# The residual kept by tokens in a two-block transformer kernel on one NeuronCore

## The reference

```
x = x + scale * gate * rmsnorm(sublayer(rmsnorm(x, g_in) [* (1+sc) + sh]), g_out)
rmsnorm(x, g) = x / sqrt(mean(x*x over the 1024 features) + eps) * g
order: FFN, attention+SSD, FFN | FFN, RWKV-7 time mix, FFN | gated conv, MoE, delta net, MoE
```

## Time and profile before

| | |
|---|---|
| three executions | 3096.75 us median, 3092.67 to 3099.21 |
| the profiled execution | 3096.22 us, its span 3094.4 us |
| busy in the span | PE 92%, PEld 73%, DVE 42%, ACT 36%, POOL 7% |
| mean granted TensorE clock | 0.955 |
| DMA | 695.31 MB, mean 225 GB/s |

### The profile page before, as it was taken

One profiled execution on the slowest core, in us unless ns is written; L12 is line 12 of the kernel. 1 busy time (PEld: TensorE's weight loads), 2 busy tenths in 40 slices (PEclk: granted clock), 3 DMA queues, 4 the chain that ended last, 5 costly groups with the idle time before them and its releaser, 6 DMA issues.

```text
span 3094.4 us, 44358 instructions
## 1 busy us (share of the span) xinstructions
PE 2850.0 (92%) x18548; PEld 2243.9 (73%) x18548; DVE 1293.7 (42%) x2083; ACT 1121.7 (36%) x1980; POOL 205.5 (7%) x174
## 2 busy tenths in 40 slices
PE   8999878998999998789998999999896979999998
PEld 6879656887878888578797666666695856666665
DVE  5556266546447544455464121212384442212212
ACT  5444245435447222254443122222454242222222
POOL 1000001001000212110010000000102400000000
PEclk9999898999999999899998999999897989999999
DMA  8424655535525111054243799999550035999996
GB/s 339 180 96 164 260 232 226 193 137 190 191 83 204 56 55 55 28 202 179 109 164 150 310 417 418 415 416 414 225 186 14 1 122 227 415 415 417 414 416 252
DMA packets 95540, 695.31 MB, mean 225 GB/s; under 512 B 10592, under 2 KB 10720, under 8 KB 11232
## 3 DMA queue, kind: packets, MB, share of 16 engines
q1 hardware_dynamic: 95328, 692.33, 56.4%
HBM read 691.23 MB, written 1.05 MB: 224 GB/s over the span
## 4 chain that ended last, share of the span: by engine, by line
PE 86%; DVE 5%; ACT 4%; issue 2%; DMA 1%; POOL 0%; SPq 0%; DVEq 0%; ACTq 0%
PE bank L1486 14%; PE bank L741 12%; PE bank L743 12%; PE bank L742 12%; PE bank L1546 7%; PE bank L1464 4%; PE bank L1573 4%; PE bank L1826 2%; PE bank L1834 2%; PE bank L1838 2%; DMA weight_ring<-weight_slots 1%; PE bank L1370 1%; PE bank L1936 1%; PE bank L575 1%; PE bank L2342 1%
## 5 line engine op out<-in xcount | busy, mean ns | idle before, releaser
L1486 PE MATMUL bank<-weight_ring,packed_h 128*64 128x256 f32 x2176 | 285.4, 379 | 0.0
L741 PE MATMUL bank<-source_hi_lo,weight_hi_lo 128*128 128x256 f32 x864 | 253.8, 294 | 11.9 <-DVE source_hi_lo L731 4.9
L1486 PE MATMUL bank<-more_slots,packed_h 128*64 128x256 f32 x1920 | 257.0, 379 | 1.5 <-ACT packed_h L1473 1.5
L741 PE MATMUL bank<-gate_up_hi_lo,x_hi_lo 128*128 128x512 f32 x640 | 254.0, 397 | 0.0
L1486 PEld LDWEIGHTS bank<-weight_ring,packed_h 128*64 128x64 f32 x2176 | 196.5, 137 | 74.0 <-issue 18.1
L743 PE MATMUL bank<-gate_up_hi_lo,x_hi_lo 128*128 128x512 f32 x640 | 249.7, 390 | 0.0
L742 PE MATMUL bank<-gate_up_hi_lo,x_hi_lo 128*128 128x512 f32 x640 | 249.2, 389 | 0.0
L742 PE MATMUL bank<-source_hi_lo,weight_hi_lo 128*128 128x256 f32 x864 | 248.0, 287 | 0.0
L743 PE MATMUL bank<-source_hi_lo,weight_hi_lo 128*128 128x256 f32 x864 | 247.8, 287 | 0.0
L1486 PEld LDWEIGHTS bank<-more_slots,packed_h 128*64 128x64 f32 x1920 | 174.1, 137 | 69.6 <-issue 15.4
L700 DVE TENSOR_TENSOR weight_hi_lo<-weight_ring,weight_hi_lo 128x1024 fp32r<-128x1024 f32 x138 | 168.1, 1222 | 103.9 <-ACT weight_hi_lo L694 103.9
(11 more groups left out here) (546 smaller groups left out, 5548.4 us busy)
## 6 DMA issues: line engine op xcount, KB each, us to landing
weight_ring<-weight_slots SPq DMA_DIRECT2D x437, 1024.0 KB, 7.5
more_slots<-weight_slots SPq DMA_DIRECT2D x212, 1024.0 KB, 9.3
params_sb<-small_params SPq DMA_DIRECT2D x1, 3216.5 KB, 17.8
h_sb<-weight_slots SPq DMA_DIRECT2D x3, 1024.0 KB, 4.9
y_sb<-weight_slots SPq DMA_DIRECT2D x3, 1024.0 KB, 8.3
x_sb<-x_T SPq DMA_DIRECT2D x1, 1024.0 KB, 4.8
out_T<-x_sb SPq DMA_DIRECT2D x4, 256.0 KB, 2.1
params_sb<-small_params SPq DMA_DIRECT2D x1, 73.5 KB, 4.6
```

The costliest lines, as they stand in the source:

```text
L741: e.matmul(out, w[0], x[0], start=start, stop=False, skip_group_check=shared)
L1486: mm = e.matmul(ps[x * CAP:(x + 1) * CAP, m * FB:(m + 1) * FB], self.hc[:, c, (2 * (p % 2) + x) * CAP:(2 * (p % 2) + x + 1) * CAP], wt[:, ...
```

## The change

x lies by tokens (128 x 2 x 1024). y times its inverse times the norm's weights, which now are a row spread over all partitions, is one DVE instruction for each bank, and a second adds it to x. The squares of x are summed along the free axis by ACT in one instruction for each 128 tokens. At the head of each stage PE turns x (FFN) or x times its inverse (others), and ACT (chunks 0 to 3) and DVE (chunks 4 to 7) read the turned x from banks 6, 7, 0 and 1, in pieces of 128x128, with gain and shift applied there.

The rows of weights come as six more slots of 1 MB (`plan_gain`) in the first six stages; in the last four PE spreads them and ACT writes them (`spread_pe`, `spread_act`), before `out_rows_pe` in conv and delta, and before the first gather in MoE. The place of a gain slot is free for the next load when the stage's x is whole (`x_new` of q = 1, f = 1). `out_rows_pe` makes its last two chunks first for banks 0 and 1, then for 2 and 3. The FFN head splits both halves of its first weights on ACT between the pieces of x, and all low parts on DVE. POOL's work at the FFN heads and in delta's (L3567) is gone, and so are `back_pe`, `early_act`, `chunk_act` and the norm's products on PE. The diff, cut to its new lines (the old ones stand above):

```diff
+def gain_slot(g):
+    row = np.zeros((P, SLOT), np.float32)
+    row[:, 0:D] = g
+    return row
...
+        slots.append(gain_slot(a["norm_gains"][layer, 1]))
...
+        self.x, self.h, self.y = sb("x_sb", [P, TT, D]), sb("h_sb", [P, C, T]), sb("y_sb", [P, C, T])
+        by_tokens = lambda m: m[:, :, :].rearrange("p c t -> p (c t)").rearrange("p (q d) -> p q d", q=TT)
+        self.y_tok, self.h_tok = by_tokens(self.h), by_tokens(self.y)
...
+    def x_T(self, q, c):
+        return self.k.bank[(6, 7, 0, 1)[2 * q + c // 4]][:, c % 4 * P:c % 4 * P + P]
+    def turn_in_pe(self, e, src, came, read):
+        k, n = self.k, self.n
+        for q in range(TT):
+            for c in range(C):
+                if c % 4 == 0:
+                    if q == 0:
+                        k.banks.take(e, (n, "turned", c // 4), *read(c + 3), of=(6 + c // 4,))
+                    for signal in came(q, c // 4):
+                        e.wait_ge(*k.ge(*signal))
+                mm = e.transpose(self.x_T(q, c), src[:, q, c * P:(c + 1) * P], k.par("ident"))
+                if c % 4 == 3:
+                    mm.then_inc(*k.up("in_turned", n, q, c // 4))
+    def squares_act(self, e, q):
+        k, n = self.k, self.n
+        if n:
+            e.wait_ge(*k.ge(*self.x_key(q, 1)))
+        e.activation(k.y_tok[:, q, :], k.x[:, q, :], ACT.Square, accum_out=k.x_sums[:, q:q + 1]).then_inc(*k.up("x_squared", n, q))
+        e.wait_ge(*k.ge("x_squared", n, q))
+        e.activation(k.x_dev[:, q:q + 1], k.x_sums[:, q:q + 1], ACT.Sqrt, scale=1.0 / D, bias=k.par("eps", 0, 1)).then_inc(*k.up("x_deviation", n, q))
+    def inverse_of_x_dve(self, e, q):
+        k, n = self.k, self.n
+        e.wait_ge(*k.ge("x_deviation", n, q))
+        e.reciprocal(k.x_inv[:, q:q + 1], k.x_dev[:, q:q + 1]).then_inc(*k.up("x_inverse", n, q))
+    def head_act(self, e):
+        k, n = self.k, self.n
+        for q in range(TT):
+            self.squares_act(e, q)
+            e.wait_ge(*k.ge("x_inverse", n, q))
+            e.activation(k.h_tok[:, q, 0:512], k.x[:, q, 0:512], ACT.Copy, scale=k.x_inv[:, q:q + 1]).then_inc(*k.up("scaled_first", n, q))
+            if q == 0:
+                self.begin(e)
+                self.first_split_act(e)
+    def first_split_act(self, e):
+        self.split_act(e, 0)
+    def first_half_dve(self, e):
+        self.scaled_dve_half(e, 0)
+    def head_dve(self, e):
+        self.scaled_dve_half(e, 1)
+        self.begin(e)
+    def scaled_dve_half(self, e, q):
+        k, n = self.k, self.n
+        self.inverse_of_x_dve(e, q)
+        e.wait_ge(*k.ge("x_inverse", n, q))
+        e.tensor_scalar(k.h_tok[:, q, 512:1024], k.x[:, q, 512:1024], k.x_inv[:, q:q + 1], None, ALU.mult).then_inc(*k.up("scaled_second", n, q))
...
+    def h_key(self, c, q=1):
+        return "h_second" if c // 4 else "h_first", self.n, q, c
     def norm_pe(self, e):
+        n = self.n
+        self.turn_in_pe(e, self.k.h_tok, lambda q, f: (("scaled_second" if f else "scaled_first", n, q),), lambda c: (self.h_key(c, 0),))
...
+    def norm_act(self, e, gain, shift=None, behind=None, between=None):
+        k, n = self.k, self.n
+        for q in range(TT):
+            if q == 0:
+                e.wait_ge(*k.ge("x_squared", n, 1))
+            e.wait_ge(*k.ge("in_turned", n, q, 0))
+            for c in range(4):
+                if shift is None:
+                    e.activation(k.h[:, c, q * P:(q + 1) * P], self.x_T(q, c), ACT.Copy, scale=gain[:, c:c + 1]).then_inc(*k.up(*self.h_key(c, q)))
+                else:
+                    e.activation(k.h[:, c, q * P:(q + 1) * P], self.x_T(q, c), ACT.Identity, scale=gain[:, c:c + 1], bias=shift[:, c:c + 1]).then_inc(*k.up(*self.h_key(c, q)))
+                if q and behind and c:
+                    behind(c - 1)
+            if q == 0 and between:
+                between()
         if behind:
+            for c in range(3, C):
+                behind(c)
+    def norm_dve(self, e, gain, shift=None, behind=None):
+        k, n = self.k, self.n
+        for q in range(TT):
+            e.wait_ge(*k.ge("in_turned", n, q, 1))
+            for c in range(4, C):
+                if shift is None:
+                    e.tensor_scalar(k.h[:, c, q * P:(q + 1) * P], self.x_T(q, c), gain[:, c:c + 1], None, ALU.mult).then_inc(*k.up(*self.h_key(c, q)))
+                else:
+                    e.tensor_scalar(k.h[:, c, q * P:(q + 1) * P], self.x_T(q, c), gain[:, c:c + 1], shift[:, c:c + 1], ALU.mult, ALU.add).then_inc(*k.up(*self.h_key(c, q)))
+        if behind:
             for c in range(C):
+                behind(c)
+    def plan_gain(self):
+        w = self.k.weights
+        self.gain_at = w.take()
+        self.gain_row = w.mem(self.gain_at)[:, 0:D]
+        w.done(self.gain_at, ("x_new", self.n, 1, 1))
+    def gain_in(self):
+        return self.k.weights.landed(self.gain_at)
...
+    def spread_pe(self, e, gain):
+        k, n = self.k, self.n
+        for f in range(2):
+            ps = k.banks.take(e, (n, "gain", f), ("gain_row", n, f))
+            for c in range(4 * f, 4 * f + 4):
+                mm = e.matmul(ps[:, c % 4 * P:c % 4 * P + P], gain[:, c:c + 1].to_broadcast([P, P]), k.par("ident"), start=True, stop=True)
+            mm.then_inc(*k.up("gain_spread", n, f))
+    def spread_act(self, e):
+        k, n = self.k, self.n
+        for f in range(2):
+            e.wait_ge(*k.ge("gain_spread", n, f))
+            e.activation(self.gain_row[:, f * 512:f * 512 + 512], k.banks.at(n, "gain", f)[:, :], ACT.Copy).then_inc(*k.up("gain_row", n, f))
     def back_act(self, e, scale=1.0):
         k, n = self.k, self.n
...
         for q in range(TT):
             for b in (2 * q, 2 * q + 1):
                 e.wait_ge(*k.ge(*self.y_key(b)))
+                e.activation(k.y_tok[:, q, b % 2 * 512:b % 2 * 512 + 512], k.bank[b][:, :], ACT.Square, accum_out=k.y_sums[:, b:b + 1]).then_inc(*k.up("out_squared", n, b))
             e.wait_ge(*k.ge("out_squared", n, 2 * q + 1))
             e.wait_ge(*k.ge("out_part", n, q))
             e.activation(k.y_dev[:, q:q + 1], k.y_sums[:, 2 * q + 1:2 * q + 2], ACT.Sqrt, scale=s2, bias=k.y_part[:, q:q + 1]).then_inc(*k.up("out_deviation", n, q))
         nxt = self.following()
         if nxt:
+            nxt.head_act(e)
+    def back_dve(self, e, gain_in, scale=1.0):
         k, n = self.k, self.n
         s2 = 1.0 / (scale * scale)
         nxt = self.following()
...
             e.wait_ge(*k.ge("out_deviation", n, q))
             e.reciprocal(k.y_inv[:, q:q + 1], k.y_dev[:, q:q + 1]).then_inc(*k.up("out_inverse", n, q))
             e.wait_ge(*k.ge("out_inverse", n, q))
+            for f in range(2):
+                cut = slice(f * 512, f * 512 + 512)
+                if q == 0:
+                    e.wait_ge(*gain_in(f))
+                e.scalar_tensor_tensor(out=k.y_tok[:, q, cut], in0=k.bank[2 * q + f][:, :], scalar=k.y_inv[:, q:q + 1], in1=self.gain_row[:, cut],
+                                       op0=ALU.mult, op1=ALU.mult).then_inc(*k.up("out_scaled", n, q, f))
+            if nxt and q:
+                nxt.first_half_dve(e)
+            for f in range(2):
+                cut = slice(f * 512, f * 512 + 512)
+                e.wait_ge(*k.ge("out_scaled", n, q, f))
+                e.tensor_tensor(k.x[:, q, cut], k.x[:, q, cut], k.y_tok[:, q, cut], ALU.add).then_inc(*k.up("x_new", n, q, f))
         if nxt:
+            nxt.head_dve(e)
...
     def out_rows_pe(self, e, first, tag, chunks=C):
         k, n = self.k, self.n
+        def part(kc, b, end):
+            w = self.units[first + kc][2]
+            tq, cut = slice(b // 2 * P, b // 2 * P + P), slice(b % 2 * 512, b % 2 * 512 + 512)
+            x = self.x_r[:, :, kc, tq]
+            return self.mm3(e, k.bank[b][:, :], (x[:, 0, :], x[:, 1, :]), (w[:, 0, cut], w[:, 1, cut]), kc == 0, end)
+        for kc in range(chunks - 2):
+            e.wait_ge(*k.ge(*self.lo_key(first + kc)))
             e.wait_ge(*k.ge("source_lo", n, tag, kc))
             for b in range(4):
+                mm = part(kc, b, False)
+            mm.then_inc(*k.up("unit", n, first + kc))
+        for q in range(TT):
+            for kc in (chunks - 2, chunks - 1):
+                if q == 0:
+                    e.wait_ge(*k.ge(*self.lo_key(first + kc)))
+                    e.wait_ge(*k.ge("source_lo", n, tag, kc))
+                for b in (2 * q, 2 * q + 1):
+                    mm = part(kc, b, kc == chunks - 1)
+                    if kc == chunks - 1:
+                        mm.then_inc(*k.up("y_done", n, b))
...
+    def head_act(self, e):
+        k, n = self.k, self.n
         self.begin(e)
+        for q in range(TT):
+            self.split_gate_up_act(e, q)
+            for c in range(C):
+                if c % 4 == 0:
+                    e.wait_ge(*k.ge("in_turned", n, q, c // 4))
```

(31 more changed lines are left out.)

304 lines of the change are left out of this document (82 added, 222 removed).

## The result

The changed kernel takes 3058.82 us in the median (3057.0 to 3061.29, four runs) against 3097.03 (3092.67 to 3099.21, four runs): a ratio of 0.9878 with a 95% interval of 0.9862 to 0.9893, 33 to 43 us less. The forecast was 3068 with a range of 3054 to 3088. The profiled execution took 3057.37 us, its span 3055.5, so the spans fell by 38.9 us.

What follows compares the result with a forecast made beforehand. PE was taken to bound the kernel (86% of the chain), so only the seams could gain. Terms 18 + 5 + 4.1 + 3 + 1.3 - 2.9 = 28.5 us, off 3096.5, gave 3068, range 3054 to 3088.

Steps and rivals of the forecast that it cites:

- FFN heads: Three seams before an FFN: last y product to PE's own pace falls from 24.1 to 18.1 us, 18 us in all.
- q = 0 is ready 1.3 us earlier: Stage tails with the new order of rows: the first 128 tokens' y is whole 1.3 us sooner.
- Attention, RWKV and conv heads: First product at T + 11.3 against 11.9, chunks then at PE's pace: 1 us each, 3 in all.
- By the timeline it ends as POOL starts, since POOL waits for ACT's split, and I take nothing.: Attention, conv, delta heads: addition to x escapes POOL's low weights; no loss counted where the contention rule gave some 1 us each.
- Delta's head: First product 14.6 us after the first Square against 18.0, then less waiting beside POOL: 5 us, bounds 3 and 7.
- MoE heads: Two heads: first router product at T + 9.2 against 12.0, plus a faster second router: 4.1 us for both.
- PE had been warmed by the norm's products (L575), which are gone, so I take 1.5 off there: Second MoE head: its router products lose the warming behind their 5.07 us, so 1.5 us less gain.
- What is added: Spreading the weights row costs 1.5 us in conv, 0.9 in delta, 0.5 for both MoE: 2.9 lost.
- Start and end: Kernel start, set by weight loads, gains 0.3 us; the last addition at the end lands 1.0 us earlier.
- The small pieces cost more than they free: Rival: extra ACT and DVE pieces at FFN heads leave 3 us each, others nothing: 3085 to 3090; chance 0.20.
- No change: Rival: waits in the first blocks behind the heads cancel the gains: 3092 to 3099 us; chance 0.06.
- Slower: the clock: Rival: PE idles in the seams, so the nine heads run at low clock: 3100 us and more; chance 0.06.

Runs made afterwards that it cites:

- e0: The changed kernel again, nothing edited, for a second profile: 3056.28 us, ratio 0.9872.
- e8: Kernel before the change, with DVE instead of POOL making the low weights of the first half at the four FFN heads: 3094.05 us, ratio 0.9991.
- e1: Changed kernel with `out_rows_pe` back to the old order of rows, all eight chunks with the four banks in turn: 3064.46 us, ratio 0.9895.
- e7: Changed kernel with the low weights of the first half back on POOL at the four FFN heads: 3075.61 us, ratio 0.9922.
- e3: Changed kernel with the second unit's low weights on DVE, not POOL, at the attention, conv and delta heads: 3055.63 us, ratio 0.9873.
- e2: Changed kernel with DVE's first half of q = 1's sum of squares (`out_part`) ahead of q = 0's additions: 3053.63 us, ratio 0.9864.
- e9: Changed kernel with the edits of e2, e3 and e6 together: 3047.52 us, ratio 0.9836.
- e6: Changed kernel with ACT's copies of the spread weights behind the output source's high parts in conv and delta: 3058.51 us, ratio 0.9871.
- e5: Kernel before the change, plus 16 unused PE transposes ahead of the first gather of both MoE stages: 3095.59 us, ratio 0.9994.
- e4: Changed kernel plus unused PE transposes in the gaps of the heads: 3053.36 us, ratio 0.9858.
- e10: e9 plus the unused PE transposes of e4: 3049.93 us, ratio 0.9844.

## Why the prediction was right, and its sizes

**FFN heads: 18 forecast, 22.7 measured (21.2 in e0).** The times along the head of FFN 3 were right: first product at T + 5.2 forecast and T + 4.74 measured, end of the 32 high products at 14.5 and 13.75, pace at 18.1 and 17.2. The mis-sized term is "24.1 - 18.1 = 6.0 us, and three such heads give 18": the earlier trace rows are an FFN to FFN seam, while the two behind attention and RWKV had taken 25.2. That gives 2.1 of the missing 4.7 us; the rest is the 0.9 us by which each head was quicker. Where it comes from is shown in parts: 2.3 us a head is DVE freed from POOL (e8), 2.5 us behind attention and RWKV is the order of rows (e1), which the sum had only as "q = 0 is ready 1.3 us earlier". The parts don't simply add (the same low weights on POOL cost 5 us in the changed kernel, e7), and no run takes the remaining 3.0 to 4.6 us a head apart; the timelines show only that the first product comes at T + 4.7 to 5.5 where it came at T + 8.8 to 9.8.

**Attention, RWKV and conv heads: 3 less forecast, 0.8 more measured.** Attention's and conv's are 0.4 and 0.5 us longer in both profiles. RWKV's is 0.2 shorter here and 3.1 in e0, so that the three together are 2.2 less there. The failed step is "By the timeline it ends as POOL starts, since POOL waits for ACT's split, and I take nothing." It looked at the addition alone, and for that it was right: the additions end at 212.08 and POOL starts at 212.23. It left out what comes after. The chain of waits of attention's head in the changed kernel (start, length, what) shows an instruction that POOL holds, L801, and the late `out_part`:

```profile
208.19 0.07 DVE out_part L708
...
208.35 0.30 ACT out_deviation L697
...
208.88 1.41 DVE h_sb L716 x2
...
210.39 0.49 DVE y_sb L593
210.88 1.21 DVE x_sb L723 x2
...
212.12 1.16 ACT h_sb L559 x2
...
213.83 0.73 ACT y_sb L574
...
214.60 1.98 PE bank L550 x8
...
216.61 1.13 DVE h_sb L654 x4
217.74 1.51 DVE source_hi_lo L801
...
219.38 0.55 PE bank L811
```

L801 stands in the chain with 1.51 us (0.34 in e3's), and L697 waited for `out_part` until 208.35. A second one is held beside the chain, L593 of q = 1 next to POOL's first low part (212.23 to 214.59):

```profile
213.83 1.05 DVE L593 TENSOR_SCALAR y_sb<-x_sb,x_inverse 128x512 f32<-128x512 f32 x1
```

e3 gave 1.2 us back at each head and e2 0.4; with both (e9) attention's first product stands at T + 10.8 and conv's at T + 11.0, where T + 11.3 was forecast. The rule that was weighed and set aside, the contention of the Trainium skill (GPSIMD Engine Reference, specifications), stood: e7's additions (5.19 for 1.28) are what it says of two inputs in SBUF.

**Delta's head: 5 forecast, 4.6 measured.** The first product came 15.96 us after the first Square (14.6 forecast, 18.03 before); the missing 1.3 is POOL again (e3: 14.88 for 16.18). Of the units behind it 2.4 us were gained. POOL's 8.29 us of the earlier trace rows are gone there, and the clock in the first 8 us was 0.62 for 0.51; how much of the gain is whose, no run separates.

**MoE heads: 4.1 forecast, 8.1 measured.** The router's first product was forecast at T + 9.2 and came at 9.4 and 9.5. The router's 16 products:

```profile
1638.42 4.38 PE L1301 MATMUL bank<-h_sb,params_sb 128*73 128x256 f32 x16
...
2502.19 4.28 PE L1301 MATMUL bank<-h_sb,params_sb 128*73 128x256 f32 x16
```

They take 4.4 and 4.3 us for 6.62 and 5.07. The step "PE had been warmed by the norm's products (L575), which are gone, so I take 1.5 off there" failed: without them both routers are faster than either was. Of the 8.1 us 5.0 are the earlier first product (5.6 forecast) and 3.0 the router's own. Why its clock is higher stays open. That the turn of q = 1, which ends where the router begins, does what the norm's products did, is no rule: in e1 the same turn stood there, and the router's products took 5.5 and 5.3 us.

**What is added: 2.9 forecast.** Conv's spread cost 0.8 us where 1.5 was forecast and delta's 1.2 for 0.9 (e6); conv's units took 1.1 us less before it, so that its body gained. The MoE spreads were put at 0.5 for both and gave 3.4 (e5 shows 3.0 of it).

**Start and end.** 0.3 and 1.0 forecast, 0.35 and 0.65 measured.

**Not forecast.** The FFN bodies took 3.6 us more and attention's body 4.6 less. e0 has the four FFN bodies 0.9 us above those of before and attention 1.9 below, and the FFN bodies of all profiles are 176.9 to 177.3 us without a dip of the clock in them and 178.3 to 179.9 with one, so most of this is where a dip falls. It comes to 1 us together, and the spans' 38.9 stand against a sum of 28.5 mainly by the FFN heads (4.7), the MoE heads (4.0), the MoE bodies (3.9) and conv's body (2.0), less the three heads that gave nothing (3.8). The total of 3058.8 us lies 9 below the forecast and near the fast end of its range; that it isn't further off is partly luck, as the misses run both ways.

**The rivals.** "The small pieces cost more than they free" is out: the sixteen pieces took 0.27 us each on DVE and 0.27 to 0.28 on ACT. "No change" is out too: behind the three FFN heads PE isn't idle once from the first product to 30 us after the pace is regained. "Slower: the clock" had the place right and the sign wrong: the clock in the FFN seam rose from 0.79 to 0.90. That it rose because PE begins sooner is argued; e1, with a later start and a lower clock, fits it. e4 and e10 show the size of the whole matter: with the clock up all through the heads 3 to 5 us are gained, or nothing. The Trainium skill (TensorE: Matmul & The Clock Gate, Why this matters for your kernels) counsels against longer idle gaps between bursts of products. e5 agrees where PE itself is the bound behind the gap (1.4 and 1.6 us a MoE body); where DVE and ACT are, filling the gaps gained 3 to 5 us in all (e4) or nothing (e10).

## What to carry to other kernels

Read which operands of a DVE instruction lie in SBUF before giving GpSimd work beside it: one low part of 2.35 us on POOL cost the critical chain 1.2 us, as much as DVE needs to make it (1.21), and two of them cost 5 us at an FFN head. In a tail that alternates between two engines, order each engine's instructions by what the other one waits for, however small they are; and finish the first half of the output early even if the whole ends no sooner. Fill PE's wait with work it needs anyway where PE is the bound behind it, size each seam from its own rows and not from one taken as typical, and take a second profile before you explain a single stretch.

## What the runs showed of the hardware that was not expected

A DVE instruction with two inputs in SBUF did not share with POOL but waited: two additions, 1.28 us alone, took 5.19 beside POOL's two instructions (5.10), and each ended 0.5 to 0.6 us after one of them. Also one with a single tensor input and its output in SBUF (L593, 0.49) took 1.05 beside POOL, while L654, with its input in PSUM, kept its time (1.13 and 1.11 for four).

With more products in attention's head (PE busy 8.09 us of 13 for 4.57) the clock stayed at its upper level for all of it, mean 1.00 for 0.60, and fell only when the dense products had begun (0.57 from 220 to 224 us, PE busy 4.00 of 4.00). The same program had RWKV's seam at 14.3 or at 17.2 us from one execution to another.
